# Expert weights moved in transfers of 2 MB instead of 1 MB in a mixture-of-experts decoder trunk

## What is computed

```python
gu = xs @ w_gu[e] + b_gu[e]
gate, up = gu[:, :D_FF], gu[:, D_FF:]
gate = jnp.minimum(gate, SWIGLU_LIMIT)
up = jnp.clip(up, -SWIGLU_LIMIT, SWIGLU_LIMIT)
act = gate * jax.nn.sigmoid(SWIGLU_ALPHA * gate) * (up + 1)
return act @ w_dn[e] + b_dn[e]
```

## Time and profile before

| | |
|---|---|
| median of 3 runs | 1274.71 us (1274.35 to 1274.89) |
| span of the profiled execution | 1273.4 us (1.3 us less than the median) |
| TensorE matmul busy | 978.5 us, 77% |
| TensorE weight load busy | 618.9 us, 49% |
| VectorE, ScalarE busy | 452.8 us, 351.5 us |
| DMA | 469.56 MB, mean 369 GB/s |
| expert weight transfers | 384 of 1024 KB |

### The profile page before, as it was taken

One profiled execution on the slowest core, in us unless ns is written; L12 is line 12 of the kernel. 1 busy time (PEld: TensorE's weight loads), 2 busy tenths in 40 slices (PEclk: granted clock), 3 DMA queues, 4 the chain that ended last, 5 costly groups with the idle time before them and its releaser, 6 DMA issues.

```text
span 1273.4 us, 30534 instructions
## 1 busy us (share of the span) xinstructions
PE 978.5 (77%) x12639; PEld 618.9 (49%) x12640; DVE 452.8 (36%) x1085; ACT 351.5 (28%) x735; POOL 8.4 (1%) x20
## 2 busy tenths in 40 slices
PE   6999999975995897956779947587877774664665
PEld 3889989742552554533435524343544342331332
DVE  0565465633343343432224412323233322322212
ACT  1553434512233232331113312213232221211113
POOL 0100000000000000000000000000000000000000
PEclk9999999988997898987889968888888897877779
DMA  9989578989999999999999699999889999999994
GB/s 360 369 287 338 209 286 296 320 327 407 408 407 406 408 360 408 408 407 408 408 409 374 256 373 403 407 408 408 326 312 408 408 408 406 407 407 409 408 408 177
DMA packets 128897, 469.56 MB, mean 369 GB/s; under 512 B 8156, under 2 KB 9220, under 8 KB 125668
## 3 DMA queue, kind: packets, MB, share of 16 engines
q1 hardware_dynamic: 128740, 467.07, 93.9%
HBM read 466.00 MB, written 1.05 MB: 367 GB/s over the span
## 4 chain that ended last, share of the span: by engine, by line
PE 49%; SPq 23%; issue 13%; DMA 12%; DVE 2%; ACT 1%; DVEq 0%; ACTq 0%
PE B L1182 25%; SPq L346 23%; PE B L941 12%; DMA W<-in_w_down_dram 9%; PE B L1190 3%; DMA raw<-in_w_in_dram 2%; PE B L1198 2%; PE B L1139 2%; PE B L961 2%; PE B L1145 1%; DMA raw<-in_w_ada_dram 1%; ACT wh L453 0%; PE B L968 0%; DVE wl L654 0%; PE B L1244 0%
## 5 line engine op out<-in xcount | busy, mean ns | idle before, releaser
L1182 PE MATMUL B<-W,mT 128*32 128x256 f32 x8832 | 571.3, 407 | 57.1 <-DMA W<-in_w_down_dram 19.8
L1182 PEld LDWEIGHTS B<-W,mT 128*32 128x32 f32 x8832 | 309.1, 118 | 295.7 <-issue 79.4
L1190 PE MATMUL B<-b_gu,mT 128*32 128x256 f32 x736 | 73.1, 447 | 210.3 <-issue 210.3
L571 ACT ACTIVATE hT<-hT 32x256 bf16<-32x256 bf16 x368 | 152.5, 415 | 223.6 <-DVE hT L885 215.7
L1190 PEld LDWEIGHTS B<-b_gu,mT 128*32 128x32 f32 x736 | 24.8, 119 | 237.4 <-issue 227.6
L864 DVE TENSOR_SCALAR EW<-B 128x256 f32<-128x256 f32 x46 | 19.4, 423 | 288.3 <-PE B L1182 288.3
L941 PE MATMUL B<-hh,wh 128*128 128x256 f32 x384 | 109.9, 286 | 0.0
L941 PE MATMUL B<-hl,wh 128*128 128x256 f32 x384 | 108.6, 283 | 0.0
L941 PE MATMUL B<-hh,wl 128*128 128x256 f32 x384 | 108.6, 283 | 0.0
L560 ACT ACTIVATE EW<-EW 128x256 f32<-128x256 f32 x46 | 19.1, 416 | 298.0 <-DVE EW L864 297.9
L654 DVE TENSOR_TENSOR wl<-raw,wh 128x2048 fp32r<-128x2048 f32 x32 | 72.8, 2313 | 71.5 <-ACT wh L453 71.5
(11 more groups left out here) (205 smaller groups left out, 717.4 us busy)
## 6 DMA issues: line engine op xcount, KB each, us to landing
W<-in_w_gate_up_dram SPq DMA_DIRECT2D x256, 1024.0 KB, 18.5
W<-in_w_down_dram SPq DMA_DIRECT2D x128, 1024.0 KB, 18.3
raw<-in_w_in_dram SPq DMA_DIRECT2D x13, 2048.0 KB, 9.1
raw<-in_w_ada_dram SPq DMA_DIRECT2D x12, 2048.0 KB, 12.7
raw<-in_w_out_dram SPq DMA_DIRECT2D x2, 2048.0 KB, 10.0
raw<-in_w_in_dram SPq DMA_DIRECT2D x2, 1024.0 KB, 12.1
x_sb<-in_x_dram SPq DMA_DIRECT2D x1, 1024.0 KB, 4.9
out_dram<-HV SPq DMA_DIRECT2D x4, 256.0 KB, 2.5
```

The source lines that it names most:

```text
L571: A(ys[CAP * m:CAP * m + CAP, g * QC:(g + 1) * QC], yp[CAP * g:CAP * g + CAP, m, :], ACT.Copy).then_inc(y_moved, 1)
L1182: t = M(dst[CAP * g:CAP * g + CAP, 0:QC], src[:, k % KQ, CAP * (k // KQ):CAP * (k // KQ) + CAP], w_half(block_slot(b), k)[:, g * QC:(g + 1 ...
L1190: ts = [M(dst[CAP * g:CAP * g + CAP, 0:QC], sel[:, j0 + g // 2, :], b_gu[:, QC * (g % 2):QC * (g % 2) + QC], start=True, stop=False) for g ...
```

## The change

A block is cut in two halves of four rows k (2 MB) instead of four quarters. There are two semaphores for each place in place of four, one wait and one give-back for each half, and one transfer of 2 MB for each half. Rows, places and the order of the blocks stay. Before the experts, the loads of quarters become loads of halves at the same points, with one difference: of block 1's second half nothing is loaded early any more, and all of it waits for the routing table.

```diff
-        QUARTERS = 4
+        HALVES = 2
+        HK = KT // HALVES
...
-        s_block = [[sem(f"s_block{r}{q}") for q in range(4)] for r in range(PAIRS)]
+        s_block = [[sem(f"s_block{r}{q}") for q in range(HALVES)] for r in range(PAIRS)]
...
-        gu_v = w_gate_up[0].rearrange("e (q k p) n -> e q p k n", k=2, p=P)
-        dn_v = w_down[0].rearrange("e (q k p) n -> e q p k n", k=2, p=P)
+        gu_v = w_gate_up[0].rearrange("e (q k p) n -> e q p k n", k=HK, p=P)
+        dn_v = w_down[0].rearrange("e (q k p) n -> e q p k n", k=HK, p=P)
...
-                    sp.dma_start(w_half(block_slot(b), slice(2 * q, 2 * q + 2)), src[q]).then_inc(s_block[b % PAIRS][q], 16)
+                    sp.dma_start(w_half(block_slot(b), slice(HK * q, HK * q + HK)), src[q]).then_inc(s_block[b % PAIRS][q], 16)
...
-            load(0, 0, (2, 3))
-            sp.wait_ge(sp_done, NG // 2)
-            load(1, 0, (2,))
+            load(0, 0, (1,))
...
             sp.wait_ge(table_ready, 1)
-            load(1, 0, (3,))
+            load(1, 0, (1,))
             with sp.Fori(0, TURNS) as i:
                 for b in range(PAIRS, PAIRS + 3 * TURN):
-                    for q in range(QUARTERS):
-                        sp.wait_ge(released, QUARTERS * (3 * TURN * i + b - PAIRS) + q + 1)
+                    for q in range(HALVES):
+                        sp.wait_ge(released, HALVES * (3 * TURN * i + b - PAIRS) + q + 1)
                         load(b, TURN * i + b // 3, (q,))
...
-                    if k % 2 == 0:
-                        pe.wait_ge(s_block[b % PAIRS][k // 2], 16 * uses)
+                    if k % HK == 0:
+                        pe.wait_ge(s_block[b % PAIRS][k // HK], 16 * uses)
...
-                    if done and k % 2 == 1 and k < KT - 1:
+                    if done and k % HK == HK - 1 and k < KT - 1:
                         t.then_inc(released, 1)
```

More of the change, by code:

```diff
@@ L340, in _, with load @@
                     sp.dma_start(b_dn[0:E, :], b_down[0]).then_inc(s_bdn, 16)
-            def load(b, e, qs=range(4)):
+            def load(b, e, qs=range(HALVES)):
                 src = (gu_v[e, :, :, :, 0:FF], gu_v[e, :, :, :, FF:2 * FF], dn_v[e, :, :, :, :])[b % 3]
                 for q in qs:
-                    sp.dma_start(w_half(block_slot(b), slice(2 * q, 2 * q + 2)), src[q]).then_inc(s_block[b % PAIRS][q], 16)
+                    sp.dma_start(w_half(block_slot(b), slice(HK * q, HK * q + HK)), src[q]).then_inc(s_block[b % PAIRS][q], 16)
@@ L348, in _ @@
             assert [n % RING for n in (NU - 3, NU - 2, NU - 1)] == [1, 2, 0]
             sp.wait_ge(split_l, SPLITS * (len(split_units) - 2))
-            load(0, 0, (2, 3))
-            sp.wait_ge(sp_done, NG // 2)
-            load(1, 0, (2,))
+            load(0, 0, (1,))
             sp.wait_ge(split_l, SPLITS * (len(split_units) - 1))
-            load(2, 0, (0, 1))
+            load(2, 0, (0,))
             sp.wait_ge(m_ready, NH * 2)
-            load(1, 0, (0, 1))
+            load(1, 0, (0,))
@@ L357, in _ @@
             sp.wait_ge(split_l, SPLITS * len(split_units))
-            load(0, 0, (0, 1))
+            load(0, 0, (0,))
             sp.wait_ge(mix_done, TA)
-            load(2, 0, (2, 3))
-            load(3, 1, (0, 1))
+            load(2, 0, (1,))
+            load(3, 1, (0,))
             sp.wait_ge(mix_done, TA * NH)
-            load(3, 1, (2, 3))
+            load(3, 1, (1,))
             load(4, 1)
             sp.wait_ge(table_ready, 1)
-            load(1, 0, (3,))
+            load(1, 0, (1,))
@@ L367, in _ @@
             with sp.Fori(0, TURNS) as i:
                 for b in range(PAIRS, PAIRS + 3 * TURN):
-                    for q in range(QUARTERS):
-                        sp.wait_ge(released, QUARTERS * (3 * TURN * i + b - PAIRS) + q + 1)
+                    for q in range(HALVES):
+                        sp.wait_ge(released, HALVES * (3 * TURN * i + b - PAIRS) + q + 1)
                         load(b, TURN * i + b // 3, (q,))
             b = 3 * E - 1
-            for q in range(QUARTERS):
-                sp.wait_ge(released, QUARTERS * (b - PAIRS) + q + 1)
+            for q in range(HALVES):
+                sp.wait_ge(released, HALVES * (b - PAIRS) + q + 1)
@@ L375, in _ @@
                 load(b, E - 1, (q,))
-            sp.wait_ge(released, QUARTERS * (3 * (E - 2) + UP + 1))
+            sp.wait_ge(released, HALVES * (3 * (E - 2) + UP + 1))
             sp.dma_start(gfin, final_norm_g[:].partition_broadcast(P)).then_inc(s_gfin, 16)
```

## The result

The changed kernel takes 1283.23 us (median of 4 runs, 1280.71 to 1285.34), the kernel before 1274.8 us in the runs beside it: a ratio of 1.006, with an interval of 1.0043 to 1.0078. That is 7.6 us more (5.5 to 9.9); 6.3 were forecast. One execution of a later kernel took 1792.74 us at a granted clock of 0.551 and stays out of its ratio. The profiled execution is the shortest of the four, 1280.71 us with a span of 1279.0, so its trace shows 5.6 of the 7.6 us.

A forecast was written before the change was run, and what follows sets the result against it. The path alternates between TensorE and DMA, four changes each way, with DMA idle at four places. Give-backs 4.90 + landings 3.45 - transfers 2.0 = +6.3 us, on 1273.4 gives 1279.7, as a median 1281.0; range 1276 to 1288.

The forecast's parts named there:

- the four places where the work changes hands: Idle places of DMA at 266 to 272, 458 to 464, 756 to 760 and 914 to 929 us, awaiting TensorE's give-back.
- The give-backs (4.90): At DMA's four idle places SyncE's first load waits a quarter longer: 1.58, 0.86, 1.65 and 0.81, together 4.90 us.
- landings 2 and 3: TensorE's last waits for DMA at 665.93 and 867.94 us, before it becomes the late one again.
- The landings (3.45): At four last landing waits TensorE has two quarters left instead of one: 0.86 us each at full clock, 3.45 us.
- the clock rival: TensorE's legs after DMA legs begin at half clock, 2.4 us each: 1285.8, with the tail 1288.2; chance 0.10.
- Half as many transfers (-2.0): Along the path's DMA legs 145 transfers fall away, each saving a small packet of 14 ns: -2.0 us.
- The early load (0): Block 1's 1 MB moved behind the routing table, 2 MB issued at about 260.7 us: costs DMA nothing.
- the third restart: SyncE's first issue after DMA's idle place at 756 to 760 us; its give-back comes 1.65 us later, at half clock.
- Hidden by the ring: Rival: W's 20 MB hide delayed releases and landings, only packets count: 1272.7, no change that can be told; chance 0.12.
- Uneven engines: Rival: late DMA engines lag by a cost per transfer, half of which goes: faster, 1271.6; chance 0.09.
- Branches: Rival: instruction pages wait for whole transfers, up to 2.6 us at six TensorE branches: +15.5, 1296.5; chance 0.05.

The follow-up runs named there:

- the first set: The changed kernel's first runs, beside the kernel before: 1283.23 against 1274.8 us, ratio 1.006.
- the two repeats: The changed kernel run twice more without an edit, against the kernel before: 1284.44 us, ratio 1.0077, and 1284.23 us, ratio 1.0067.
- the third set: The changed kernel unedited, run a third time, beside its version in 1 MB transfers and the unchanged kernel before: 1284.23 us, ratio 1.0067.
- the first pair: First profiles of the kernel before and the changed kernel, set side by side piece by piece: +5.6 us in total.

## Why the prediction was right, and where it was not

The direction and the mechanism were right: the ring hides neither gate at the four places where the work changes hands. The size, 6.3 us, lies in the interval of the first set (5.5 to 9.9), but just below those of the two repeats (7.5 to 12.2 and 6.5 to 10.5): the forecast is low by some 2 us, and that the first set came out lowest is luck. The steps one by one:

*The give-backs (4.90)*: shown by the kernel that has them alone, +4.2 (2.4 to 6.0). The four places hold; the third stayed the last place where DMA runs low ahead of landing 3 in every profile. What is less sure is its size. The 1.65 us are a quarter at half clock, and TensorE was at half clock there in the kernel before (0.50), but at 1.00 in the first profile of the changed kernel, where a quarter takes 0.86 us, and at 0.50 again in the third set.

*The landings (3.45)*: shown, but mis-sized: +5.2 (3.4 to 6.9) alone. All four last waits have 32 matmuls behind them. The tail, which is free of other changes, grew by 0.87 in the first pair and 0.83 in the second: 0.86 was right at full clock. What was left out of the sum is what two quarters cost when the wait ends at half clock, 3.47 and 3.58 us in place of 1.93, against 1.93 in place of 1.07 for one. At landings 2 and 3 TensorE was at half clock, for all or part of them, in 7 of 12 cases in the six profiles with the coarse wait, and in 6 of 10 in the five with quarters. The change thus doesn't bring the low clock about, as the clock rival had it, but pays more each time that it is there: 3.3 us on average for the 32 matmuls (1.4 above full clock) against 1.85 for 16 (0.8 above). Over the two landings of a run this makes some 0.7 us. The prediction had this as an edge of the range.

*Half as many transfers (-2.0)*: the step that failed. A fixed 14 ns for every packet, solved from two mixes of packet sizes, was taken for the price of a transfer's end; what else differs between the mixes must have gone into it, though no run shows what. With the small packets halved, 300 us brought 121.66 MB in the first profile of the changed kernel and 121.36 in the third, beside 121.46 and 121.53 before: no gain that is steady. The four pieces of DMA show +1.5 and -0.2 us. The Trainium skill, "DMA: Bandwidth & Descriptors", section "Anatomy of one DMA — SWDGE (gpsimd) path", which calls the semaphore bubble tiny (for transfers that GpSimd issues; here SyncE issues them), was nearer for this change, as the sum without the term. Going down to 512 KB did cost something, 3.2 us (1.7 to 4.8), of which DMA's pieces show 1.8; whether the rest is the transfers' or scatter was not settled.

*The early load (0)*: 1.0009, nothing that can be told; up to 2.8 us is not excluded by that run. DMA lost nothing by it, as said. The prediction looked only at DMA and at the cover of block 1, and passed over TensorE's stand in "issue" at 270 us, which the late load can lengthen (0.3 to 3.4 us with it in two transfers, 0.9 to 1.1 in the changed kernel).

With these corrections the sum is 4.9 + 3.45 + 0.7 + 0 = 9.0 us, or 8.3 with the third restart at full clock. The three ratios of the changed kernel give 7.6, 9.8 and 8.5. The shares of the corrections are worked out from single profiles and are an argument, not a measurement; the two gates and the absent gain of the transfers are measured.

*The rivals.* Hidden by the ring fell with the two gates run alone. Uneven engines: DMA's share in the two stretches that end with the last landing is 0.79 and 0.46 with half the transfers, 0.72 and 0.43 before, and twice the transfers cost 3.2 us where 57 ns for each would have made 17: it fell. Clock: above. Branches: 6064 ns in the median, 6852 at the most, beside 6059 and 6711 before; had a page of instructions waited for whole transfers, up to 2.6 us more would stand there. The rule that the Trainium skill gives in "DMA: Bandwidth & Descriptors", section "Queues, rings and completion order", that an engine changes queues at packets, agrees with it.

## What to carry to other kernels

In a stream that DMA bounds, look for the few places where a full buffer leaves DMA idle and where the consumer hangs on the last byte; each such change of hands costs one piece of the consumer's work, so the piece by which loads are waited for and places are given back is set by these, and apart from the size of a transfer. Find the restart that counts by asking after which one DMA has no gap any more up to the next landing, and ask it in stretches of a microsecond or two over all of that time: a dip that seems gone can have moved by a few microseconds. Making the ends finer pays only if the next piece comes free in time too: a transfer that restarts DMA must last until the next give-back.

## What had not been expected of the hardware

Between transfers of 0.5, 1 and 2 MB the rate of a full stretch does not change to the eye: 121.50, 121.46 to 121.53, and 121.36 to 121.66 MB in 300 us. And the same kernel, unchanged, scattered from 1271.2 to 1279.5 us over its runs, with 49 equal matmuls at 5.61 us in one of its profiles and 4.65 in another: by how much of them ran at the lower clock, the pieces of one pair of profiles differ by more than the steps that were forecast. And TensorE's stand in "issue" behind the first 14 matmuls took 0.3 us in both profiles of the kernel before, where DMA was empty, and 2.6 to 3.5 us in the four where DMA was still at work.
